# Joined U and V rows gathered into one ring, and routing cut into runs, in a one-core expert layer

## The reference, cut to what matters

```
s1 = q[:, :, 0] @ k1.T ; s2 = q[:, :, 1] @ k2.T        # per head, 128 keys each
v1, i1 = top_k(s1, 16) ; v2, i2 = top_k(s2, 16)
sc, ci = top_k(v1[:, None] + v2[None, :], 16)
expert = i1[ci // 16] * 128 + i2[ci % 16]
a = einsum(u_tab[expert], xn)                           # one row of 1024 floats per expert
wgt = softmax(sc) * gelu(a)
y = einsum(wgt, v_tab[expert])                          # a second row of 1024 floats
```

## Time and profile before

| | us |
|---|---|
| median of 3 runs | 1902.95 |
| lowest and highest run | 1885.69, 1908.68 |
| the profiled execution, its own time | 1893.19 |
| span of its trace | 1891.4 |

### The profile page before, as it was taken

The page is one execution under the profiler, slowest core; times in us unless marked ns, Lnnn a source line. Parts: engine busy times, 40 slices in busy tenths (PEclk is TensorE's granted clock), DMA queues, the critical chain, the costliest instruction groups (busy, mean ns, idle before and its releaser), DMA issues.

```text
span 1891.4 us, 14658 instructions
## 1 busy us (share of the span) xinstructions
PE 1479.6 (78%) x4385; PEld 627.8 (33%) x4385; DVE 1053.2 (56%) x2673; ACT 376.1 (20%) x899; POOL 1214.5 (64%) x1291
## 2 busy tenths in 40 slices
PE   7973787889699676778986767799767777777789
PEld 4451464333144222223442222244322222222233
DVE  4843413885958954444698444447964444444430
ACT  2342232121122221111121111112221111111111
POOL 0007400577777777777677777777777777777763
PEclk9986678899899999999999999999999999999999
DMA  8036053779899899999989999999999999999996
GB/s 321 30 74 159 26 229 112 256 245 376 324 351 348 317 359 372 398 409 410 409 297 344 376 367 403 409 410 344 347 362 407 405 409 410 409 410 409 409 395 231
DMA packets 171054, 618.34 MB, mean 327 GB/s; under 512 B 19728, under 2 KB 25184, under 8 KB 169984
## 3 DMA queue, kind: packets, MB, share of 16 engines
q0 software_dynamic: 156928, 571.18, 78.9%
q1 hardware_dynamic: 14048, 46.22, 7.2%
HBM read 610.52 MB, written 5.19 MB: 326 GB/s over the span
## 4 chain that ended last, share of the span: by engine, by line
POOL 23%; PE 23%; DVE 15%; DMA 13%; issue 9%; ACT 1%; DVEq 0%
PE sb_peer_acc L1548 18%; POOL sb_peer_U L1188 12%; DMA sb_kept_V<-peer_v,sb_kept_expert 11%; POOL sb_kept_V L1197 11%; DVE sb_peer_U L1354 4%; PE sb_peer_pq L1473 4%; DMA sb_peer_U<-peer_u,sb_kept_expert 1%; DVE sb_peer_hot L1289 1%; DVE sb_peer_f L1292 1%; DVE sb_peer_idx L1241 1%; DVE sb_peer_idx L1233 1%; DVE sb_peer_left L1234 1%; DVE sb_peer_val L1238 1%; DVE sb_peer_hot L1291 1%; DVE sb_peer_val L1230 1%
## 5 line engine op out<-in xcount | busy, mean ns | idle before, releaser
L1548 PE MATMUL sb_peer_acc<-sb_kept_V,sb_peer_dg 128*128 128x512 f32 (+1 forms) x2176 | 1048.7, 617 | 315.7 <-DMA sb_kept_V<-peer_v,sb_kept_expert 220.9
L1354 DVE CUSTOM_DVE_ANT_0 sb_peer_U<-sb_peer_U,sb_rows_xn 128x1024 f32<-128x1024 f32 x512 | 620.1, 1225 | 547.7 <-DMA sb_peer_U<-peer_u,sb_kept_expert 536.9
L1548 PEld LDWEIGHTS sb_peer_acc<-sb_kept_V,sb_peer_dg 128*128 128x128 f32 (+1 forms) x2176 | 379.4, 188 | 960.8 <-issue 498.6
L1197 POOL DMA_INDIRECT sb_kept_V<-peer_v,sb_kept_expert x512 | 543.2, 1061 | 170.1 <-issue 108.5
L1188 POOL DMA_INDIRECT sb_peer_U<-peer_u,sb_kept_expert x512 | 526.5, 1028 | 186.8 <-issue 151.1
L1430 ACT ACTIVATE sb_peer_dg<-sb_kept_ident,sb_peer_wt 128x128 f32<-128x128 f32 (+1 forms) x544 | 210.7, 395 | 1070.7 <-PE sb_peer_acc L1548 842.6
L1188 POOL DMA_INDIRECT sb_peer_U<-peer_u,sb_peer_es x32 | 40.5, 1267 | 143.9 <-DVE sb_peer_es L1293 122.4
L1473 PE MATMUL sb_peer_pq<-sb_rows_wq,sb_peer_xnT 128*128 128x512 f32 x256 | 114.2, 600 | 1.1 <-ACT sb_peer_xnT L1382 1.1
L467 PE MATMUL sb_proj_pz<-sb_proj_w_in,sb_proj_xT 128*128 128x512 f32 (+1 forms) x192 | 71.7, 534 | 8.8 <-DVE sb_proj_xT L299 8.8
L630 POOL MEMSET sb_rows_wq<- 16x4096 f32 x1 | 3.5, 3506 | 116.6 <-POOLq L162 116.6
L1473 PEld LDWEIGHTS sb_peer_pq<-sb_rows_wq,sb_peer_xnT 128*128 128x128 f32 x256 | 49.0, 193 | 63.8 <-issue 62.3
(11 more groups left out here) (259 smaller groups left out, 990.8 us busy)
## 6 DMA issues: line engine op xcount, KB each, us to landing
sb_peer_U<-peer_u,sb_kept_expert POOLq DMA_INDIRECT x512, 6.6
sb_kept_V<-peer_v,sb_kept_expert POOLq DMA_INDIRECT x512, 6.6
sb_proj_w_in<-w_in SPq DMA_DIRECT2D x8, 640.0 KB, 10.8
sb_kept_V<-w_out SPq DMA_DIRECT2D x1, 4096.0 KB, 15.2
sb_proj_xT<-xT SPq DMA_DIRECT2D x8, 272.0 KB, 9.7
sb_proj_x<-x_tok SPq DMA_DIRECT2D x4, 512.0 KB, 12.4
sb_proj_w_mem<-w_mem SPq DMA_DIRECT2D x1, 2048.0 KB, 19.7
sb_blend_MT<-sb_rows_wq SPq DMA_DIRECT2D x8, 256.0 KB, 10.0
```

Of the source, the lines that this page charges most:

```text
L1197: pool.indirect_dma_start(V[:, m % RV, :], None, d["peer_v"], bass.IndirectOffsetOnAxis(ap=rows(m), axis=0)).then_inc(s_v[m % RV], 16)
L1354: dve.tensor_tensor_reduce(U[:, n % RU, :], U[:, n % RU, :], x, 1.0, 0.0, ALU.mult, ALU.add, a[:, g % 2, n % GRP:n % GRP + 1]).then_inc(s_ ...
L1548: mm = pe.matmul(acc[:r, c, :], dg[:, n % RD, 0:r], V[:, n % RV, c * 512:(c + 1) * 512], start=(s == 0), stop=(s == count[k] - 1))
```

## The change

- The host joins the tables: `peer_uv` has rows of 2048 floats, U then V. One gather per step brings 128 rows of 8 KB into one of ten slots (six in `UVb`, four in the memory that `w_out` used). Gather `n` waits for the matmuls of step `n - 10`; gather 6 waits for all output projections.
- ACT takes the gelu of one column per step, multiplies it with the gate column, and makes the diagonal at once; DVE's `weights` is gone, and there is no lag between dot and matmuls.
- A part is routed per 32 steps: its queries start 36 steps ahead of its first step, one accumulating matmul per step; `best`, `sums` and `numbers` follow 15, 18 and 21 steps behind that, `gates` 23. `turn` of the next tile comes at step 76 of a tile.
- `acc` is doubled (even and odd tiles), the score banks go from four to two, `qT`, `rowq`, `ex`, `expert` and `gate` become small rings.
- At the start half of `project(1)` comes ahead of `turn(0)`, the rest of the projections directly behind the decode tile's scores, and `turn(1)` and the first queries after them; ACT does all five norms ahead of the first step.

```diff
-        RU, RV, RD = 7, 8, 4
+        RB, RA, RD, RW = 6, 4, 4, 16
+        R = RB + RA
...
+        query = {(k, b): max(0, first[k] + QS * b - 36) for k in range(1, NT) for b in range(4)}
+        ROWS_OUT, QTURN, QUERY_OUT, SCORE = 9, 10, 12, 13
+        BEST, SUMS, EXPS, NUMBERS, GATES = 15, 18, 20, 21, 23
+        TURN, TURN_OUT = 76, 78
+        RESIDUAL = (0, 3, 5)
+        RESULT = 4
...
+        out_banks = [acc[0][:, :, :], acc[1][:, :, :], acc[0][:, :, :], acc[1][:, :, :], psc[:, :, :]]
...
+                for n in range(NS):
                     k, s = steps[n]
+                    if s % QS == 0:
+                        pool.wait_ge(s_id, part(k, s // QS) + 1)
+                    if n == RB:
+                        pool.wait_ge(s_om, NT)
+                    if n >= R:
+                        pool.wait_ge(s_mm, n - R + 1)
+                    at = part(k, s // QS) % 4
+                    pool.indirect_dma_start(slot(n).rearrange("p e c -> p (e c)"), None, d["peer_uv"],
+                                            bass.IndirectOffsetOnAxis(ap=expert[:, at, s % QS:s % QS + 1], axis=0))\
+                        .then_inc(s_uv[n % R], 16)
...
+                    for kb in due(n, BEST):
+                        best(*kb)
+                    for kb in due(n, SUMS):
+                        sums(*kb)
+                    for kb in due(n, NUMBERS):
+                        numbers(*kb)
...
+                    dve.wait_ge(s_uv[n % R], 16 * (n // R + 1))
+                    u = slot(n)[:, 0, :]
+                    dve.tensor_tensor_reduce(u, u, K.xn[:, order[k], :], 1.0, 0.0, ALU.mult, ALU.add,
+                                             a[:, n % RW:n % RW + 1]).then_inc(s_dot, 1)
...
+                    w = slice(n % RW, n % RW + 1)
+                    act.wait_ge(s_dot, n + 1)
+                    act.activation(ga[:, w], a[:, w], ACT.Gelu).then_inc(s_ga, 1)
+                    if s % QS == 0:
+                        act.wait_ge(s_gt, part(k, s // QS) + 1)
+                    act.wait_ge(s_ga, n + 1)
+                    act.activation(wt[:, w], ga[:, w], ACT.Copy,
+                                   scale=gate[:, part(k, s // QS) % 4, s % QS:s % QS + 1]).then_inc(s_wt, 1)
                     if n >= RD:
                         act.wait_ge(s_mm, n - RD + 1)
...
+                    act.wait_ge(s_wt, n + 1)
+                    act.activation(dst, src, ACT.Copy, scale=wt[:, w]).then_inc(s_dg, 1)
...
+                project(1, 0)
                 turn(0)
                 sample_scores()
-                project(1)
+                project(1, 1)
+                pe.wait_ge(s_h, 1)
+                project(2, 0)
+                project(2, 1)
+                pe.wait_ge(s_h, 2)
+                project(3, 0)
+                project(3, 1)
+                pe.wait_ge(s_sr, 1)
+                project(4, 0)
+                project(4, 1)
                 turn(1)
-                queries(1, 0)
-                turn_queries(1, 0)
-                scores(1, 0)
-                for j in range(2, NT):
-                    project(j)
...
+                    for c in range(KD):
+                        for kb in due(n, c):
+                            queries(*kb, c)
...
+                        mm = pe.matmul(acc[k % 2][:r, c, :], dg[:, n % RD, 0:r], slot(n)[:, 1, c * 512:(c + 1) * 512],
                                        start=(s == 0), stop=(s == count[k] - 1))
...
-        "peer_u": A["peer_u"][0],
-        "peer_v": A["peer_v"][0],
+        "peer_uv": np.concatenate([A["peer_u"][0], A["peer_v"][0]], 1),
```

More of the change, by code:

```diff
@@ L1086, in part, with slot @@
             return b if k == 0 else 1 + 4 * (k - 1) + b
+        def slot(n):
+            m = n % R
+            return UVb[:, m, :, :] if m < RB else UVa[:, m - RB, :, :]
+        expert = S.sb("expert", [P, 4, QS], U32)
+        gate = S.sb("gate", [P, 4, QS])
         xnT = S.sb("xnT", [P, KD, P])
-        qT = S.sb("qT", [P, NH2, P])
+        qT = S.sb("qT", [P, 4, P])
         iota = S.sb("iota", [P, TOPK], BF16)
         ss = S.sb("ss", [P, NT])
-        rowq = S.sb("rowq", [P, 2, 4 * P])
+        rowq = S.sb("rowq", [P, 4 * P])
         val = S.sb("val", [P, 4, TOPK])
@@ L1127, in experts @@
         s_gt = S.sem("gates_known")
-        s_u = [S.sem(f"u_landed{n}") for n in range(RU)]
-        s_v = [S.sem(f"v_landed{n}") for n in range(RV)]
+        s_uv = [S.sem(f"rows_landed{n}") for n in range(R)]
         s_dot = S.sem("dots")
@@ L1227, in best @@
                     dve.wait_ge(s_sc, n + 1)
-                    sc = [psc[:r, b, m * P:(m + 1) * P] for m in range(4)]
+                    sc = [psc[:r, n % 2, m * P:(m + 1) * P] for m in range(4)]
                     for m in range(4):
@@ L1347, in _ @@
                         result(k - 1)
[L1348 to L1354, removed]
-                                             a[:, g % 2, n % GRP:n % GRP + 1]).then_inc(s_dot, 1)
-                for g in range((NS - 1 - WEIGH) // GRP + 1, NG):
-                    weights(g)
+                    dve.wait_ge(s_uv[n % R], 16 * (n // R + 1))
+                    u = slot(n)[:, 0, :]
+                    dve.tensor_tensor_reduce(u, u, K.xn[:, order[k], :], 1.0, 0.0, ALU.mult, ALU.add,
+                                             a[:, n % RW:n % RW + 1]).then_inc(s_dot, 1)
                 result(NT - 1)
@@ L1534, in _ @@
                     r = ROWS[order[k]]
-                    if k and k + 1 < NT and s == 0:
+                    if 0 < k < NT - 1 and s == TURN:
                         turn(k + 1)
-                    for kb in due(n, 0):
-                        queries(*kb)
+                    for c in range(KD):
+                        for kb in due(n, c):
+                            queries(*kb, c)
                     for kb in due(n, QTURN):
```

200 lines of the change are left out of this document (70 added, 130 removed).

## The result

The changed kernel takes 1745.84 us (median of 4 runs, 1745.22 to 1746.27), 0.9239 of the kernel before, with a 95% interval of 0.9201 to 0.9278. The ratio compares fast runs alone, without one run of the kernel before that took 2476.28 us. Against the three runs shown ahead, median 1902.95 us, it would be 0.917; beside the experiments the kernel before has medians of 1890.48 to 1895.89 us, which gives 0.921 to 0.923. The forecast was 1766, 20 us too long. The profiled execution took 1746.27 us, its span is 1744.5.

What follows compares the result with a forecast made beforehand. POOL's gather issue was taken as the limit where the rate is low, with PE beside it. Gather 6 landing at 381.0, 1374.7 of steps, chain 4.3, result and store 4.3, outside 1.8 gave 1766 us; range 1720 to 1840.

Steps and rivals of the forecast that it cites:

- What bounds it: Expert stage: POOL's gather issue limits where the rate is low, PE beside it where queries are packed; transfers end at 410 GB/s.
- One gather a step: POOL in the expert stage: one 8 KB-row gather takes 1 to 2 us, below 2.56, so transfers set the pace.
- The price of a step: Expert stage: time per step, taken as 2.56 us from the 410 GB/s stretch with bytes unchanged.
- the sum: Whole kernel: gather 6 landed at 381.0, 537 steps 1374.7, chain 4.3, result and store 4.3, outside 1.8: 1766 us.
- faster transfers: Rival, expert stage: 8 KB rows go at POOL's former best of 2.48 us a step, 1723 us; chance 0.08.
- The ring and routing: Expert stage: ten slots leave 13.9 us spare; DVE's three-run routing lags 6.3 us at worst, so transfers don't notice.
- The rival of a ring too short: Expert stage: spare gone, each of 16 parts shows DVE's 6.3 us lag, 101 us in all, 1867; chance 0.07.
- Queries spread, ACT's work: Expert stage: PE lags at most 2.3 us, ACT needs 0.84 of 2.56 us a step; both counted at nothing.
- The start: Before the steps: first gather at 339.7, gather 6 issued at 373.9, landed at 381.0; transfers stand still about 14 us.
- The end: After the last row lands: 4.3 us of chain replace 34 steps of V, then 4.3 us to the span's end.

Runs made afterwards that it cites:

- the plain loads: Changed kernel with gathers replaced by SP-queue loads of consecutive rows, not the routed ones: 8 KB rows 1738.29 us, two times 4 KB 1778.35 us.

## Why the prediction was right or wrong

*What bounds it.* Right. POOL was the limit: put its second gather back and the price of a step, 2.755 us, is within 1% of the kernel before, which has (1745.91 - 412.73) / 480 = 2.778 between its dots of steps 32 and 512. These two dots, then its last one and the matmuls behind it:

```profile
412.73 1.22 DVE L1354 CUSTOM_DVE_ANT_0 sb_peer_U<-sb_peer_U,sb_rows_xn 128x1024 f32<-128x1024 f32 x1
...
1745.91 1.22 DVE L1354 CUSTOM_DVE_ANT_0 sb_peer_U<-sb_peer_U,sb_rows_xn 128x1024 f32<-128x1024 f32 x1 [1.43 <-DMA sb_peer_U<-peer_u,sb_kept_expert]
...
1825.38 1.23 DVE L1354 CUSTOM_DVE_ANT_0 sb_peer_U<-sb_peer_U,sb_rows_xn 128x1024 f32<-128x1024 f32 x1 [1.32 <-DMA sb_peer_U<-peer_u,sb_kept_expert]
...
1826.78 60.32 PE L1548 MATMUL sb_peer_acc<-sb_kept_V,sb_peer_dg 128*128 128x512 f32 x140 [0.61 <-DMA sb_kept_V<-peer_v,sb_kept_expert]
```

The 110 matmuls and 47.4 us of the earlier trace rows start where that view's window starts; TensorE's last run has 140 and 60.3 us, at the same 1.72 us a step. So from the last dot to the end of the span the kernel before needs 1891.4 - 1825.4 = 66.0 us and the changed one 8.7. The run with two gathers, which has no V lag either, needs 8.6: there it is the ring. From the first gather to the last dot the changed kernel needs 1735.9 - 337.5 = 1398 us and the run with two gathers 1516: there it is the joining.

*One gather a step.* Right: 0.94 to 2.00 us but for one, and POOL waits for matmuls.

*The price of a step* is the term that was mis-sized: "Bytes are unchanged, and I take the 2.56 us of the 410 GB/s stretch." The 410 GB/s belonged to rows of 2 to 5 KB; 8 KB rows go at 421, 2.49 us. From the dot of step 6 to the last one, 537 steps took 1735.85 - 376.64 = 1359.2 us, 2.531 each with all that disturbs them: 15.5 us less than the sum's 1374.7. The rival "faster transfers" named the 2.48 that regular steps show, from POOL's former pace, which is luck; its reason, a loss between rows, fits the plain loads. As a mean over all steps 2.48 was too low. The Trainium skill (DMA: Bandwidth & Descriptors, section Why small descriptors are slow (HBM only)) spoke for it with its fixed cost for each packet, by which an estimate of 15 us was left out of the sum; the trace agrees in direction, and the plain loads show 2.8% (2.588 against 2.516) where that rule gives 1.1%. The Trainium skill's other rule there (DMA: Bandwidth & Descriptors, section SWDGE vs HWDGE vs iDMA), packets of preferably at most 4096 bytes, is not borne out here: 8 KB rows go as one packet each (78592 packets in place of 156928), and faster.

*The ring and routing.* Right, and the arithmetic holds roughly when it is bent: a lag of 14.3 us in a spare of 10 x 2.49 - 11.7 = 13.2 loses 1.3 us a part, and six slots lose 3.0 us, not 4.8. That 1.3 comes so near the foretold 1.1 is partly luck: gather 6's row landed in 5.4 us, not 7.1 (below), which would make the spare 14.9 and the loss nothing, and VectorE's waits of 1.5 us are not in the sum. The rival of a ring too short falls at ten slots and at eight.

*Queries spread, ACT's work.* Counted at nothing. Right for both, but for different reasons: the bursts would have been covered anyway, while taking the diagonals in fours costs 43 us, by the slots' longer hold and by later scores together.

*The start.* Gather 6 issued at 371.26, said 373.9; its row was there by 376.6, said 381.0: 4.4 us less. The 1.7 of them on the landing are one unloaded row's time, 5.4 us for 7.1. The 2.6 on the issue are in the main TensorE's clock: the scores end at 322.7, said 324.9. The kernel before, windows at the start and the decode tile's query matmuls:

```profile
300.00:310.00 10.00, 3.92 (x67) 2.61 (x68) 3.16 (x7) 2.73 (x4) 0.00 (x0) 0.81 0.01 2
310.00:320.00 10.00, 9.53 (x68) 2.97 (x70) 0.00 (x0) 0.39 (x1) 0.00 (x0) 0.68 0.24 52
```
```profile
311.24 9.65 PE L1452 MATMUL sb_peer_pq<-sb_rows_wq,sb_peer_xnT 128*32 128x512 f32 x64 [0.47 <-ACT sb_peer_xnT L1382]
```

and the changed kernel:

```profile
310.00:320.00 10.00, 9.11 (x76) 2.90 (x74) 0.48 (x2) 0.74 (x2) 0.00 (x0) 1.00 0.18 39
```
```profile
312.50 7.07 PE L1421 MATMUL sb_peer_pq<-sb_rows_wq,sb_peer_xnT 128*32 128x512 f32 x64 [0.47 <-ACT sb_peer_xnT L1350]
...
321.64 1.08 PE L1431 MATMUL sb_peer_psc<-sb_kept_keys,sb_peer_qT 128*32 128x128 f32 x32 [0.69 <-ACT sb_peer_qT L1359]
```

Half a projection that was counted only as 0.9 us of delay keeps TensorE busy where it had idled, and the matmuls behind it run at 2.4 GHz throughout. The gap without transfers is some 17 us and not 14 (six gathers' rows are done by 355, not 360).

*The end.* Right: 4.3 us from the last dot to 1740.2, 4.3 more to 1744.5. The sum with what was measured is 376.6 + 1359.2 + 8.7 = 1744.5 us: of the 20 us that the forecast was too long, 15.5 are the price of a step and 4.4 the start.

## What to carry to other kernels

When a resource that is at its limit is relieved, the next price must be read from rows of the new kind, or bounded by them: the ceiling of the old transfers was not that of the new ones. A ring's spare time (slots times step, less the time that a slot is held without queueing) told here which bursts on other engines cost nothing, to one or two microseconds for each part. And a gap at the start that looks like a lack of slots can be the work of an engine that stays busy behind it; fill the gap, and see where it comes out again.

## What the runs showed of the hardware

A gather of 128 rows holds POOL for 0.94 us whether the rows have 4 or 8 KB, and up to 2.00 where dots run one behind the other (1.99 with 4 KB rows). Plain loads and gathers end at the same rate, 421 GB/s with 8 KB rows, and 4 KB rows at 409 (410 when gathered). Where routing stood in one run, TensorE did nothing from 1075 to 1080 us; its granted clock was 0.50 there and 0.52 (1.2 GHz) in the next 5 us, so its first matmuls ran at that clock, when it had a backlog to work off.
